# Sixteen channel tiles of a scan computed in the seven-product form, convolved out of SBUF

## The chip, the cores and the metric

One core of a Trainium2 chip runs one program. The metric is the device time of one execution in microseconds (us), median of three runs. All data are fp32.

## The reference, cut to what matters

The program computes three hybrid blocks in a row on 512 tokens with 1024 features. The change lies in the second block's mixer, which computes (gMLP branch, then the state-space branch "ssm"):

```
u          = rmsnorm(h)
za, z, xBC, dt, gates = split(u @ w_in)            # w_in: 1024 x 9248
xBC        = silu(causal_dwconv(xBC, w, b))        # 4 taps per channel, 3072 channels
x, B, C    = split(xBC)                            # x: 2048 channels = 16 tiles of 128
y          = ssd_scan(x, dt, A, B, C) + D * x      # 32 heads of 64 channels, 4 groups for B and C
y          = rmsnorm(y * silu(z))                  # by group
uu, v      = split(gelu(za));  v = spatial mix of layernorm(v)
h          = h + (sigmoid(ga) * ((uu * v) @ w_proj_a) + sigmoid(gb) * (y @ w_proj_b)) @ w_out
```

Here a tile is 128 channels by 512 tokens. A matrix product gives tiles with channels on the partitions; the convolution then runs along the free axis, so tap n adds the tile shifted by n tokens, times a weight per partition.

## The kernel before, in words

**Layout.** Every engine has its own instruction list and they meet at semaphores. `work` is one SBUF arena of 35200 columns, `normalized` holds the eight input tiles of the mixer, `weight_ring` holds four weight slots of 1 MB (two channel tiles, that is 256 output columns, each). SyncE (SP) sends the slots in order; a slot can be sent when the one four before it has been used (`stream.used`).

**Two forms of a product.** In the direct form (`tile_pe`, L2456) one channel tile is 8 products of 128x128 weights with 512 columns. In the seven-product form (class `Sevens`, a Strassen-Winograd scheme on 2x2 blocks; job = two channel tiles) there are 7 products for each of 4 pairs of input tiles: 28 products of 256 columns in place of 32. It needs sums of weight blocks (`sums_pool`, four GpSimd instructions per slot, L999 to L1005; `token_sums_pool`, L1017 to L1022, for two slots at once), sums of input halves (`Halves`, L913 to L933), and sums of the results: `one_act` (a copy on ScalarE, L1110), `three_dve` (L1115), `five_dve` (L1122, L1124) and `all_dve` (L1129). The order of the seven is 1, 2, 6, 5, 7, 3, 4; each half bank is freed by one of these sums. Trace records count each fp32 product as two.

**The second mixer.** After dt (L2530) come eight channel tiles for B and C ("bc", direct form, banks 0 to 2) and their convolution. `convolve_dve` reads the tile from PSUM: one tensor_scalar for the first tap (L3103) and three scalar_tensor_tensor (L3106); ScalarE then applies SiLU (L2857). Then four groups: `group_pe` (L2618, L2619) with a ScalarE copy (L2786) and a masked product on VectorE (L2957); xs tile 0 stands before the first group's instructions, xs tile 1 before the third's.

**The scan's turns.** Sixteen turns follow, one per pair of heads. Turn j has three PE pieces: `turn_pe` (transposes of xs tile j, L2631), `states_pe` (L2640), `outputs_pe` (L2654, L2658). On the others: SP spreads a line of decay sums over the partitions (`spread_line`, L2418, waits for the outputs of turn j-2); GpSimd subtracts (`relative_pool`, 8 instructions, L2752) and multiplies (`weight_pool`, L2762); ScalarE takes two exponentials (`decays_act`, L2878, L2879); VectorE does `aged_dve` (L3144, both inputs in SBUF), `factors_dve` (L3121), `state_dve` (L3128, L3133) and the skip sum (L2981).

**The side work.** Between the three pieces of a turn PE runs pieces of other products, measured in units (one unit is one 256-column product; JOB = 28 units is one job). `share(slot)` says how many units have to be done by each of the 48 slots (3 per turn). The side work is xs tiles 2 to 15 in direct form (16 units each), eight gMLP jobs (`gmlp_u`, `gmlp_v`) and one job of `ssm_z`: 476 units, about 9.9 per slot. `slot_ends` and `job_ends` place the other engines' part of a tile or a job in the slot in which PE ends it, behind that slot's scan instructions. Each engine's list is in this order and is not reordered at run time. GpSimd makes the weight sums of the gMLP jobs in turns 7 to 13. After the scan come 28 more jobs (`DENSE`).

Of the kernel before, what the change touches and what calls it, by code (L numbers as in the profile page):

```python
# [20 lines left out]
P = 128  # L21
# [914 lines left out]
class Sevens:  # L936
# [8 lines left out]
    def __init__(self, K, plans, banks, sums_at, parts_at, made=None, after=None, by_token=()):  # L945
# [9 lines left out]
        self.halfway = take(sum(plan.slots // 2 for plan in by_token)) if by_token else None  # L955
# [23 lines left out]
    def weight_sum(self, n, i):  # L979
        return self.sums_at[n % 2][i]  # L980
# [6 lines left out]
    def sums_pool(self, pool, n, before_last=lambda: None):  # L987
        K, own = self.K, self.K.own_pool.of(pool)
        plan, k = self.slots[n]
        if plan in self.by_token:  # L990
            return self.token_sums_pool(pool, n)
# [15 lines left out]
    def token_sums_pool(self, pool, n):  # L1007
        K, own = self.K, self.K.own_pool.of(pool)
# [3 lines left out]
        s1, s2, s4, s3 = [bass.AP(K.work, first, [[WORK, P], [second - first, 2], [256, 2], [1, 256]]) for first, second in self.sums_at[n]] + (  # L1012
            [a21] if len(self.sums_at[n]) == 3 else [])
        for i in range(2):
            plan.wait_full(pool, 2 * k + i)
# [4 lines left out]
        pool.tensor_tensor(s3, a11, a21, ALU.subtract)  # L1020
        own.wait()
        pool.tensor_tensor(s4, a12, s2, ALU.subtract).then_inc(self.weight_sums.h, 1)  # L1022
# [9 lines left out]
    def token_job_pe(self, pe, j, source, ready):  # L1032
# [5 lines left out]
        for m, p in [(m, p) for m in self.ORDER for p in range(pairs)]:  # L1038
            if p == 0:
                self.bank_free_pe(pe, j, m)  # L1040
                if m == 6:
                    pe.wait_ge(*self.weight_sums(n + 1))
            ready(pe, m, p)
# [1253 lines left out]
TILE = 16  # L2297


class SecondMixer:  # L2300
# [3 lines left out]
    ORDER = (("bc", 8), ("xs", 16))  # L2304
# [3 lines left out]
    def __init__(self, K, d, tables, X, U, plans, sums, norm):  # L2308
# [8 lines left out]
        self.gmlp = Sevens(K, [plans["gmlp_u"], plans["gmlp_v"]], banks, self.gmlp_sums_at, parts, by_token=[plans["gmlp_v"]])  # L2317
        self.dense = Sevens(K, [plans[name] for name in self.DENSE], banks, self.weight_sums_at, parts, self.made, self.gmlp)
# [4 lines left out]
        self.u_first = ApartHalves(U, KD * TM, 0, TM, work, lambda i, p: (self.u_sums + i * 2 * T if i < 3 else self.gv + 6 * T) + p * HALF_BANK)  # L2323
# [9 lines left out]
    def places(self):  # L2333
# [15 lines left out]
        self.gmlp_sums_at = [[self.gv + (3 * (n % 2) + i) * T for i in range(3)] for n in range(4)] + [  # L2349
            [(at, at + T) for at in (self.bt, self.ct, self.cbm)],  # L2350
            [(self.w_t, self.w_t + T), (self.gv + D + T, self.gv + 3 * D + T), (self.ct + 2 * T, self.cbm + 2 * T)]]
        self.gain, self.bias, self.token_bias = (self.bt + 3 * T + i * GMLP_GROUPS * P for i in range(3))
# [6 lines left out]
    def take_signals(self):  # L2359
# [4 lines left out]
            ab0=16 * 8, ab1=16 * 8, first=12, read0=8, read1=8, read2=8, ready=24, grouped=4, copied=4, masked=4,  # L2364
# [3 lines left out]
            u_open=4, v_open=4, u_summed=3, a_summed=1, b_summed=4, out_summed=4).items()}  # L2368
# [13 lines left out]
    def sync(self, sp):  # L2382
# [86 lines left out]
    def side_pe(self, pe, start, stop):  # L2469
        for place in range(start, stop):  # L2470
            yield from self.tile_pe(pe, place)
        for j in range(len(self.gmlp.jobs)):
            source, ready = (self.u_first if j < 4 else self.u_side), {0: self.gmlp_first_pe, 4: self.gmlp_fifth_pe}.get(j, lambda pe, m, p: None)
            for _ in self.gmlp.job_pe(pe, j, source, ready):
                yield 1
        for _ in self.job_pe(pe, "ssm_z", 0):
            yield 1

    def gmlp_fifth_pe(self, pe, m, p):
        if m == 7 and p == 0:  # L2480
            pe.wait_ge(*self.s["u_summed"](3))

    def gmlp_first_pe(self, pe, m, p):
        if m in (1, 2, 5) and p == 0:
            pe.wait_ge(*self.was_read(len(self.tiles) - 3 + (1, 2, 5).index(m)))
# [10 lines left out]
    def share(self, slot):  # L2496

        total = (len(self.tiles) - self.first["xs"] - 2) * TILE + (len(self.gmlp.jobs) + 1) * JOB
# [2309 lines left out]
```

## Time and profile before

| | us |
|---|---|
| three runs: median (lowest to highest) | 3626.12 (3624.08 to 3627.43) |
| profiled execution, its own time | 3630.09 |
| profiled execution, span from first to last instruction | 3628.3 |
| PE busy | 3578.0 |
| VectorE / ScalarE / GpSimd busy | 1599.3 / 761.9 / 1495.8 |
| second mixer, B and C tiles begin | 1601.0 |
| first turn of the scan begins | 1679.2 |
| last side job's sums done, first instruction behind the scan | 1934.4 |

The page of the profile gives busy times over the whole span; the views by group, by wait, by stretch of time and in order of time show the second mixer alone. All times below are microseconds from the start of the span.

### The profile page before, as it was taken

The numbers are of one execution on the slowest core, as the hardware profiler recorded it, in microseconds if no ns is written. First come the engines' busy times: TensorE is split into PE (matmuls) and PEld (weight loads), VectorE is DVE, ScalarE is ACT, GpSimd is POOL, SyncE is SP. The second block draws the span as 40 slices with busy tenths as digits, with TensorE's granted clock in tenths as the row PEclk, the third lists the DMA queues.
The fourth block names the chain that finished last, engine by engine and source line by source line (L and its number), as shares of the span: only waits on it lengthen the run. The fifth ranks groups of instructions, "written<-read, shape, count | busy, mean of one in ns | idle before, by whom it ended". The sixth has DMA issues, their size and how long they took to land.

```text
span 3628.3 us, 45688 instructions
## 1 busy us (share of the span) xinstructions
PE 3578.0 (99%) x18937; PEld 2880.3 (79%) x18937; DVE 1599.3 (44%) x2456; ACT 761.9 (21%) x1378; POOL 1495.8 (41%) x1248
## 2 busy tenths in 40 slices
PE   8999999999999999999999999999999999899999
PEld 7888888775888888864588888888887468658888
DVE  3221222422436322135656633688623554358851
ACT  2000151223211100012334300100102454320000
POOL 4454222000645355414686664366630111026653
PEclk9999999999999999999999999999999999999999
DMA  4232444423332323231333222232223400023322
GB/s 135 82 93 75 87 70 66 74 47 76 60 74 82 93 82 91 87 99 59 105 105 100 82 82 93 82 93 82 87 87 102 81 24 5 6 78 85 90 79 76
DMA packets 370386, 286.30 MB, mean 79 GB/s; under 512 B 11283, under 2 KB 360083, under 8 KB 370180
## 3 DMA queue, kind: packets, MB, share of 16 engines
q1 hardware_dynamic: 367876, 279.44, 29.2%
q10 hardware_dynamic: 2304, 3.95, 0.4%
q8 instruction: 150, 2.46, 0.3%
q14 instruction: 56, 0.46, 0.0%
HBM read 280.64 MB, written 2.72 MB: 78 GB/s over the span
## 4 chain that ended last, share of the span: by engine, by line
PE 97%; DVE 1%; ACT 1%; issue 1%; DMA 1%; SPq 0%; DVEq 0%; ACTq 0%
PE psum L618 43%; PE psum L1078 20%; PE psum L2456 4%; PE psum L1044 3%; PE psum L3500 3%; PE psum L1704 2%; PE psum L1739 2%; PE psum L1465 2%; PE psum L4338 2%; PE psum L4073 1%; PE psum L587 1%; PE psum L3584 1%; PE psum L3604 1%; PE psum L1725 1%; PE psum L1580 1%; PE psum L3457 1%
## 5 line engine op out<-in xcount | busy, mean ns | idle before, releaser
L618 PE MATMUL psum<-work 128*128 128x256 f32 (+1 forms) x2400 | 551.4, 381 | 0.0
L537 POOL TENSOR_TENSOR work<-weight_ring 128x512 f32<-128x512 f32 x132 | 163.3, 1237 | 912.6 <-PE psum L618 732.9
L618 PEld LDWEIGHTS psum<-work 128*128 128x128 f32 x2400 | 455.9, 190 | 66.1 <-DVE work L751 0.2
L618 PE MATMUL psum<-work,weight_ring 128*128 128x256 f32 (+1 forms) x2080 | 481.8, 381 | 0.0
L618 PE MATMUL psum<-normalized,weight_ring 128*128 128x256 f32 (+1 forms) x2016 | 468.1, 382 | 3.0 <-DVE normalized L738 3.0
L618 PEld LDWEIGHTS psum<-work,weight_ring 128*128 128x128 f32 x2080 | 395.2, 190 | 57.2
L618 PEld LDWEIGHTS psum<-normalized,weight_ring 128*128 128x128 f32 x2016 | 383.8, 190 | 61.2 <-DVE normalized L738 4.3
L762 DVE TENSOR_TENSOR work<-work,psum 128x512 f32<-128x512 f32 (+1 forms) x100 | 68.6, 686 | 641.4 <-PE psum L618 641.4
L1078 PE MATMUL psum<-work,weight_ring 128*128 128x256 f32 x1216 | 283.6, 379 | 0.0
L1078 PE MATMUL psum<-work 128*128 128x256 f32 x1184 | 277.1, 379 | 0.0
L696 ACT ACTIVATE work<-psum 128x256 f32<-128x256 f32 (+1 forms) x100 | 38.5, 385 | 1094.4 <-PE psum L618 1094.4
L1078 PEld LDWEIGHTS psum<-work,weight_ring 128*128 128x128 f32 x1216 | 230.4, 190 | 31.9 <-issue 0.9
L1078 PEld LDWEIGHTS psum<-work 128*128 128x128 f32 x1184 | 224.6, 190 | 33.7 <-issue 3.7
L799 DVE SCALAR_TENSOR_TENSOR work<-work,vector_columns 128x510 f32<-128x510 f32 (+1 forms) x176 | 223.7, 1329 | 0.0
L999 POOL TENSOR_TENSOR work<-weight_ring 128x512 f32<-128x512 f32 x60 | 79.9, 1331 | 332.0 <-PE psum L1078 288.2
L542 POOL TENSOR_TENSOR work<-weight_ring,work 128x512 f32<-128x512 f32 x132 | 185.2, 1403 | 0.0
L540 POOL TENSOR_TENSOR weight_ring<-weight_ring 128x512 f32<-128x512 f32 x132 | 174.4, 1321 | 0.0
L539 POOL TENSOR_TENSOR work<-work,weight_ring 128x512 f32<-128x512 f32 x132 | 168.1, 1274 | 10.3
L2456 PE MATMUL psum<-normalized,weight_ring 128*128 128x512 f32 x384 | 170.0, 595 | 0.0
L1078 PE MATMUL psum<-normalized,weight_ring 128*128 128x256 f32 x704 | 163.5, 380 | 0.0
L618 PE MATMUL psum<-normalized,work 128*128 128x256 f32 (+1 forms) x672 | 159.9, 381 | 0.0
L1078 PEld LDWEIGHTS psum<-normalized,weight_ring 128*128 128x128 f32 x704 | 132.9, 190 | 19.4 <-issue 1.9
(556 smaller groups left out, 5317.6 us busy)
## 6 DMA issues: line engine op xcount, KB each, us to landing
weight_ring<-in_w_in SPq DMA_DIRECT2D x73, 1024.0 KB, 7.9
weight_ring<-in_w_ffn_in SPq DMA_DIRECT2D x88, 512.0 KB, 5.1
weight_ring<-in_ffn_w_up SPq DMA_DIRECT2D x44, 512.0 KB, 4.8
weight_ring<-in_ffn_up SPq DMA_DIRECT2D x44, 512.0 KB, 5.1
weight_ring<-in_w_ffn_out SPq DMA_DIRECT2D x16, 1024.0 KB, 5.2
weight_ring<-in_w_out SPq DMA_DIRECT2D x12, 1024.0 KB, 5.1
work<-decay_sums SPq DMA_DIRECT2D x16, 512.0 KB, 4.2
weight_ring<-in_w_proj_b SPq DMA_DIRECT2D x8, 1024.0 KB, 5.2
```

Of the source, the lines that this page charges most:

```text
L537: own(pool.tensor_tensor(s1, a21, a22, ALU.add))
L539: own(pool.tensor_tensor(s2, s1, a11, ALU.subtract))
L540: pool.tensor_tensor(a21, a11, a21, ALU.subtract)
L542: pool.tensor_tensor(s4, a12, s2, ALU.subtract).then_inc(self.weight_sums.h, 1)
L618: last = pe.matmul(K.ps[:, self.BANK[m] * T:self.BANK[m] * T + self.H], left(m, p), right(pe, m, p), start=first and p == 0, stop=last_par ...
L799: last = dve.scalar_tensor_tensor(out=acc[ct][:, n:T], in0=raw[ct][:, 0:T - n], scalar=weight[ct][n], in1=acc[ct][:, n:T], op0=ALU.mult, o ...
L999: own(pool.tensor_tensor(s1, a21, a22, ALU.add))
L1044: last = pe.matmul(self.half_bank(m), source.right(m, p)[:, t * P:(t + 1) * P], self.token_left(plan, k, n, m, p), start=p == 0 and m in ( ...
L1078: last = pe.matmul(self.half_bank(m), self.left(plan, k, n, m, p), source.right(m, part * pairs + p), start=first and p == 0 and m in (1, ...
L1465: last = pe.matmul(K.bank(b + h, HALF), plan.slot(k)[:, kt, ct * P:(ct + 1) * P], U[:, at:at + HALF], start=kt == 0, stop=kt == KD - 1)
L2456: last = pe.matmul(self.bank_of(place), plan.slot(k)[:, kt, ct * P:(ct + 1) * P], src[:, kt * stride:kt * stride + T], start=kt == 0, stop ...
L3500: last = pe.matmul(K.bank(4 + n % 3), plan.slot(k)[:, kt, ct * P:(ct + 1) * P], self.U[:, kt * TM:kt * TM + T], start=kt == 0, stop=kt == ...
```

## The change

All sixteen xs tiles become eight jobs of the seven-product form, in front of the gMLP jobs in one list (`self.side`, 16 jobs). Job j's four quarters go to a buffer of two tiles in SBUF (`raw`) by the usual result sums. ScalarE then computes the first tap with the bias (`begin_act`, Identity with scale and bias, from `raw` into the tile), VectorE adds the three other taps from `raw` (`taps_dve`, scalar_tensor_tensor with both tensors in SBUF, six per job), and ScalarE applies SiLU (`xs_silu_act`). Weight sums of the eight slots are added on GpSimd: slots 0 to 2 ahead of turn 0, slot j+2 in turn j up to turn 9, between `relative_pool` and `weight_pool`; the two token sums are split in two parts each. PE does 10 units of job 0 before group 0, 10 before group 2, and the rest of job 0 and 14 units of job 1 behind group 3 (`AHEAD` = 42 units) before turn 0; the remaining 434 units are spread over the 48 slots. SP sends the line of pair j behind weight slot j+2 (before: j+1).

```diff
-TILE = 16
+AHEAD = JOB + 14
-    ORDER = (("bc", 8), ("xs", 16))
+    ORDER = (("bc", 8),)
-        self.gmlp = Sevens(K, [plans["gmlp_u"], plans["gmlp_v"]], banks, self.gmlp_sums_at, parts, by_token=[plans["gmlp_v"]])
+        self.side = Sevens(K, [plans[name] for name in ("xs", "gmlp_u", "gmlp_v")], banks, self.side_sums_at, parts, by_token=[plans["gmlp_v"]])
+        self.raw = self.gu + 6 * T
@@ sync
-            if i - 1 < SSM_PAIRS:
-                self.spread_line(sp, i - 1)
+            if 3 <= i - 2 < SSM_PAIRS:
+                self.spread_line(sp, i - 2)
@@ PE
-    def side_pe(self, pe, start, stop):
-        for place in range(start, stop):
-            yield from self.tile_pe(pe, place)
...
+    def side_pe(self, pe):
+        for j in range(len(self.side.jobs)):
+            for _ in self.side.job_pe(pe, j, self.u_side, self.first_side_pe if j == 0 else lambda pe, m, p: None):
+                yield 1
+    def first_side_pe(self, pe, m, p):
         if m in (1, 2, 5) and p == 0:
+            pe.wait_ge(*self.was_read({1: 6, 2: 7, 5: 5}[m]))
@@ share, job_ends
+        return AHEAD - (-(slot + 1) * ((len(self.side.jobs) + 1) * JOB - AHEAD) // (3 * SSM_PAIRS))
+        events = dict(one=4, three=12, five=20, all=28, begin=29, open=30, taps=38, silu=46)
@@ tensor
         for g in range(SSM_GROUPS):
             if g % 2 == 0:
-                for _ in self.tile_pe(pe, xs + g // 2):
-                    pass
+                self.side_until(side, (g + 2) // 2 * 10)
             self.group_pe(pe, g)
+        self.side_until(side, AHEAD)
@@ gpsimd
+        self.relative_pool(pool, 0)
+        G.sums_pool(pool, 0)
+        pool.wait_ge(*self.plans["bc"].done(3))
+        self.u_side.last_sum(pool, 0, KD // 2).then_inc(S["u_summed"].h, 1)
+        G.sums_pool(pool, 1)
+        G.sums_pool(pool, 2)
+        self.weight_pool(pool, 0)
+        for j in range(1, SSM_PAIRS):
             self.relative_pool(pool, j)
+            if j <= 9:
+                G.sums_pool(pool, j + 2)
...
             self.weight_pool(pool, j)
@@ scalar
+    def begin_act(self, act, j):
+        S = self.s
+        act.wait_ge(*self.side.read_all(j + 1))
+        for i in range(2):
+            t = 2 * j + i
+            act.activation(self.A(self.xs + t * T, T), self.A(self.raw + i * T, T), ACT.Identity, scale=self.V("ssm_conv_w_2")(3 * 24 + t),
+                           bias=self.V("ssm_conv_b_2")(t)).then_inc(S["begun"].h, 1)
@@ vector
+        self.side_dve(dve, own, "all", 0)
+        self.side_dve(dve, own, "taps", 0)
         self.aged_dve(dve, 0)
+    def taps_dve(self, dve, own, j):
+        for i in range(2):
+            t = 2 * j + i
+            x, raw = self.A(self.xs + t * T, T), self.A(self.raw + i * T, T)
+            dve.wait_ge(*self.s["begun"](t + 1))
+            for n in range(1, 4):
+                step = dve.scalar_tensor_tensor(out=x[:, n:T], in0=raw[:, 0:T - n], scalar=self.V("ssm_conv_w_2")((3 - n) * 24 + t), in1=x[:, n:T],
+                                                op0=ALU.mult, op1=ALU.add)
+                if n < 3:
+                    own(step)
+                    own.wait()
+                else:
+                    step.then_inc(self.s["convolved"].h, 1)
```

## Rows read from the trace of the kernel before

**Rows 1.** The page: busy time and share of the span of each engine.
```profile
PE 3578.0 (99%) x18937; PEld 2880.3 (79%) x18937; DVE 1599.3 (44%) x2456; ACT 761.9 (21%) x1378; POOL 1495.8 (41%) x1248
```

**Rows 2.** Busy time by stretch: the groups, a turn with xs tiles, two with jobs.
```profile
core 0: us, PE busy (x) PEld busy (x) DVE busy (x) ACT busy (x) POOL busy (x), PEclk, DMA share, GB/s
1650.00:1700.00 50.00, 45.55 (x176) 24.29 (x175) 27.37 (x39) 11.67 (x15) 13.33 (x14) 1.00 0.15 53
1713.43:1729.29 15.86, 15.86 (x69) 8.19 (x68) 10.43 (x17) 5.83 (x6) 7.85 (x9) 1.00 0.31 94
1839.64:1855.57 15.93, 15.93 (x99) 13.89 (x98) 7.37 (x12) 4.62 (x5) 14.68 (x13) 1.00 0.28 95
```

**Rows 3.** Waits of PE, 1660 to 1940: total, times, longest.
```profile
PE psum L2631 <- ACT work L2786: 2.3, 1, 2.3
PE psum L2640 <- DVE work L3121: 2.2, 1, 2.2
```

**Rows 4.** The chain that ended last: start, length, what.
```profile
1667.43 6.88 PE psum L2456 x16
...
1860.50 0.67 PE psum L2640 x6
...
2024.53 12.09 PE psum L1078 x56
```

**Rows 5.** VectorE in order of time: the convolution of the last bc tile.
```profile
1657.95 0.81 DVE L3103 TENSOR_SCALAR work<-psum,vector_columns 128x512 f32<-128x512 f32 x1 [3.71 <-PE psum L2456]
1658.79 2.31 DVE L3106 SCALAR_TENSOR_TENSOR work<-psum,vector_columns,work 128x511 f32<-128x511 f32 x3
```

**Rows 6.** One line's instructions: duration in ns, min/median/max, first and last start.
```profile
L3106 DVE SCALAR_TENSOR_TENSOR work<-psum,vector_columns,work x72: 746/748/751, 1612.4 to 1802.5; 128x511 f32<-128x511 f32 x24, 128x510 f32<-128x510 f32 x24, 128x509 f32<-128x509 f32 x24
L799 DVE SCALAR_TENSOR_TENSOR work<-work,vector_columns x176: 734/1215/1756, 2342.7 to 3498.4; 128x511 f32<-128x511 f32 x88, 128x510 f32<-128x510 f32 x88
L3144 DVE TENSOR_TENSOR work<-work x16: 1214/1902/2547, 1682.6 to 1911.4; 128x1024 f32<-128x1024 f32 x16
L2762 POOL TENSOR_TENSOR work<-work x16: 2352/2358/2366, 1681.6 to 1909.6; 128x1024 f32<-128x1024 f32 x16
L2752 POOL TENSOR_SCALAR work<-work x128: 704/712/1687, 1640.1 to 1907.7; 128x128 f32<-128x128 f32 x128
L999 POOL TENSOR_TENSOR work<-weight_ring x60: 1265/1271/2256, 463.9 to 2296.7; 128x512 f32<-128x512 f32 x60
```

**Rows 7.** VectorE and GpSimd in order of time in turn 9.
```profile
1832.32 2.36 POOL L2762 TENSOR_TENSOR work<-work 128x1024 f32<-128x1024 f32 x1 [1.17 <-ACT work L2878]
1833.22 2.54 DVE L3144 TENSOR_TENSOR work<-work 128x1024 f32<-128x1024 f32 x1 [1.99 <-ACT work L2879]
1834.63 2.26 POOL L999 TENSOR_TENSOR work<-weight_ring 128x512 f32<-128x512 f32 x1
```

**Rows 8.** The feed-forward block's convolution from SBUF beside GpSimd's weight sums.
```profile
2507.55 3.42 DVE L799 SCALAR_TENSOR_TENSOR work<-work,vector_columns 128x511 f32<-128x511 f32 x2
2507.31 1.44 POOL L540 TENSOR_TENSOR weight_ring<-weight_ring 128x512 f32<-128x512 f32 x1
2508.72 1.72 POOL L542 TENSOR_TENSOR work<-weight_ring,work 128x512 f32<-128x512 f32 x1
2510.39 1.18 POOL L550 TENSOR_TENSOR work<-work 128x256 f32<-128x256 f32 x1
```

**Rows 9.** VectorE groups by line and shape: busy, mean ns, idle before.
```profile
L1115 DVE TENSOR_TENSOR work<-work,psum 128x512 f32<-128x512 f32 x60 | 41.1, 685 | 166.9 <-PE psum L1078 131.8 <-PE psum L1044 29.6 <-ACT work L1110 5.4
L1129 DVE TENSOR_TENSOR work<-work,psum 128x512 f32<-128x512 f32 x52 | 35.7, 686 | 75.8 <-PE psum L1078 64.2 <-PE psum L1044 11.0
L2981 DVE SCALAR_TENSOR_TENSOR work<-work,psum 128x512 f32<-128x512 f32 x16 | 11.8, 740 | 4.7 <-PE psum L2658 4.7
L3121 DVE TENSOR_TENSOR work<-psum,work 128x512 f32<-128x512 f32 x32 | 20.5, 682 | 10.6 <-PE psum L2631 10.6
```

**Rows 10.** Waits of GpSimd, 1640 to 1940: total, times, longest.
```profile
POOL work L2752 <- DMA work<-decay_sums: 33.9, 10, 6.5
```

More of the change, by code:

```diff
@@ L954, in __init__ @@
         self.read_all = take(self.results)
-        self.halfway = take(sum(plan.slots // 2 for plan in by_token)) if by_token else None
+        self.halfway, self.token_sums = (take(sum(plan.slots // 2 for plan in by_token)) if by_token else None for _ in range(2))
     def job(self, plan, c=0):
@@ L2496, in share @@
     def share(self, slot):
-        total = (len(self.tiles) - self.first["xs"] - 2) * TILE + (len(self.gmlp.jobs) + 1) * JOB
-        return -(-(slot + 1) * total // (3 * SSM_PAIRS))
-    def slot_ends(self):
-        start, stop = self.first["xs"] + 2, len(self.tiles)
-        out = {}
-        for n, place in enumerate(range(start, stop)):
-            out.setdefault(self.slot_of((n + 1) * TILE), []).append(place)
-        return out
+        return AHEAD - (-(slot + 1) * ((len(self.side.jobs) + 1) * JOB - AHEAD) // (3 * SSM_PAIRS))
     def slot_of(self, unit):
@@ L2512, in job_ends @@
     def job_ends(self, kinds):
-        first = (len(self.tiles) - self.first["xs"] - 2) * TILE
-        out = sorted((first + j * JOB + at, kind, j) for j in range(len(self.gmlp.jobs))
-                     for kind, at in dict(one=4, three=12, five=20, all=28, open=30).items() if kind in kinds)
+        events = dict(one=4, three=12, five=20, all=28, begin=29, open=30, taps=38, silu=46)
+        skip = lambda kind, j: kind == "open" if j < 8 else kind in ("begin", "taps", "silu")
+        out = sorted((j * JOB + at, kind, j) for j in range(len(self.side.jobs)) for kind, at in events.items()
+                     if kind in kinds and not skip(kind, j) and j)
         return [(self.slot_of(unit), kind, j) for unit, kind, j in out]
@@ L2868, in gelu_act @@
         A, S = self.A, self.s
-        act.wait_ge(*self.gmlp.read_all(j + 1))
+        act.wait_ge(*self.side.read_all(8 + j + 1))
         at = self.gmlp_at(j)[0]
@@ L2962, in vector @@
         own.wait()
+        self.side_dve(dve, own, "all", 0)
+        self.side_dve(dve, own, "taps", 0)
         self.aged_dve(dve, 0)
-        ends, jobs = self.slot_ends(), self.job_ends(("three", "five", "all"))
+        ends = self.job_ends(("three", "five", "all", "taps"))
         for slot in range(3 * SSM_PAIRS):
@@ L2972, in vector @@
                 self.aged_dve(dve, j + 1)
-            for place in ends.get(slot, []):
-                self.convolve_dve(dve, own, place)
-            for at, kind, job in jobs:
+            for at, kind, job in ends:
                 if at == slot:
-                    self.gmlp_dve(dve, kind, job)
+                    self.side_dve(dve, own, kind, job)
             if slot % 3 == 2:
@@ L3049, in open_dve, with side_dve @@
             dve.tensor_tensor(y, y, A(self.result(j) + (t % 2) * T, T), ALU.mult).then_inc(S["opened"].h, 1)
-    def gmlp_dve(self, dve, kind, j):
-        G, (c11, c12, c21, c22) = self.gmlp, self.gmlp_at(j)
+    def side_dve(self, dve, own, kind, j):
+        G = self.side
+        c11, c12, c21, c22 = self.gmlp_at(j - 8) if j >= 8 else [self.raw + i * HALF_BANK for i in range(4)]
         if kind == "three":
```

127 lines of the change are left out of this document (66 added, 61 removed).

## Prediction

> **What bounds the kernel now.** I read the page first, then the stretches, the waits, the chain and the instructions in order of time. The page shows PE busy for 3578.0 of 3628.3 us [rows 1]; in the stretches of the scan it is busy for the whole of 15.86 and 15.93 us, at the full granted clock [rows 2]. So a turn costs what PE has to issue in it, and the other engines cost nothing as long as they deliver in time. The only waits of PE between the B and C tiles and the end of the scan are 2.28 us at the first transposes and 2.18 us at the first states [rows 3], the 4.45 us that PE is short in 1650 to 1700 [rows 2]. The reader should see a second thing in the same rows: in a turn with jobs GpSimd is busy for 14.68 of 15.93 us, in one with xs tiles for 7.85 of 15.86 [rows 2]. VectorE has 7.4 to 10.4 us.
>
> **PE's products.** A tile in direct form takes 6.88 us, a job of two tiles 12.09 [rows 4]. Two tiles become one job: 2 x 6.88 - 12.09 = 1.67 us, times eight: 13.4 us off PE. Clock and weight loads stay as they are in both rows.
>
> **The head.** Both waits of [rows 3] go, since PE now has 22 units behind group 3: -4.46. A new one comes: the second product of job 0 takes bank 1, which VectorE reads until the last B/C tile is convolved. That convolution ends 0.2 + 0.81 + 2.31 us and small gaps, some 3.4, behind the tile's last product [rows 5]; PE has four units, 1.73 us, to cover it: +1.7. Net -2.8. Behind this wait stand only PE's own groups, which nobody needs earlier. Weight sum 0 and both halves' sums are made on GpSimd while the B/C tiles run, so product 6 doesn't wait.
>
> **The turns, PE alone.** A unit is 12.09 / 28 = 0.432 us. A turn with jobs has 99 records in 15.93 us; 38 are its own (4, 6 and 28), the rest is 30 units: 12.95. So its own pieces cost 2.98. With 434 / 16 = 27.1 units the new turn is 14.69 us, and from the end of one job to the end of the next (28 units) PE needs 14.69 x 28 / 27.1 = 15.2. That is no further gain, only the same 13.4 told by turns; it is the pace that the others must keep.
>
> **ScalarE.** Per job one copy, two first taps and two SiLUs are some 3 us; it has 4.6 to 5.9 us per turn now [rows 2]. Far from the bound, and the first tap moved there takes 2 x 0.81 us off VectorE. Nothing on the path.
>
> **SP.** The line of pair j goes one slot later in SP's list. The send in front of it waits for job j-2, which ends before the outputs that the line waits for anyway. GpSimd waits for such lines now, up to 6.5 us, ten times [rows 10], and PE waits for nothing: cost 0. If the cover went, it would be that wait less GpSimd's slack.
>
> **GpSimd.** Per turn 8 x 0.70 + 2.36, plus four weight sums of 1.27: 5.6 + 2.4 + 5.1 = 13.0 us of 14.7 [rows 6]. Before, turns 0 to 6 had only 7.9. That fits, if nobody holds it up.
>
> **VectorE's taps are the term that decides.** Read alone, a tap from PSUM is 0.748 us and one with both inputs in SBUF 0.734 at its shortest [rows 6]: even. But the second kind has a median of 1.215 and a maximum of 1.756 [rows 6]. Rows 7 and 8 show why. An instruction of VectorE with two inputs in SBUF waits while GpSimd works on SBUF and the other way round: L3144 (1.21 alone) took 2.54, ending 1.1 us behind L2762; L999 (1.27 alone) took 2.26, since it stood behind L3144 [rows 7]. Where both have a queue they alternate: two taps in 3.42 us beside L540 and L542, which grow to 1.44 and 1.72 [rows 8], so 1.68 from tap to tap. VectorE's evictions (one input in PSUM) keep 0.685 [rows 9]. The 42 PSUM taps of the scan's tiles were immune to this; the new 48 SBUF taps aren't. Their prices: 1.68 beside a 128x512 sum; beside L2762 0.73 + 2.36 less the overlap of 0.33 that 1.68 against 0.74 + 1.27 shows, 2.8; beside L2752 0.73 + 0.71 - 0.33 = 1.1.
>
> What stands beside them: the end of job j releases VectorE's last sum of it and GpSimd's weight sums for slot j+2 at once. VectorE does that sum (0.68) and `aged_dve` (1.21, with a wait 1.6), then six taps; GpSimd is by then in its second or third sum, and goes on to L2762 and the eight L2752. So three taps at 1.68, one at 2.8, two at 1.1: 10.1 us instead of 4.6.
>
> **The loop.** Behind the taps stand, on the same engine, the first sum of the next job (0.64), the skip sum (0.74) and the two instructions of `factors_dve` (1.28) [rows 9]; PE's `states_pe` waits for these. It is 0.67 [rows 4], and behind it job j+1 lacks 5 (j = 0) to 11 (j = 7) units: states of turn j come at unit 51 + 27.1j, the job ends at 56 + 28j. At eight that is 3.45. Round: 0.68 + 1.6 + 10.1 + 0.64 + 0.74 + 1.28 + 0.67 + 3.45 = 19.2 us, against 15.2 that PE needs. PE stalls 4.0 us per job, in front of `states_pe` or `outputs_pe`, for the eight jobs with taps: +32. From turn 8 on there are none, and the turn is 14.7.
>
> **Sum.** -13.4 - 2.8 + 32 = +15.8. The profiled execution's 3630.1 becomes 3645.9; its own time is 4.0 above the median of the runs, so 3642.
>
> **The bounds of the tap.** At 0.73 each (plus handover 0.04) the loop is 13.3 us, under 15.2, and PE doesn't stall. It begins to stall at 1.0 us per tap, and the change comes out even at a stall of 2.0, that is 1.35 per tap. The mean over all 176 of L799 is just 1.33, but the feed-forward stages leave GpSimd free for half of each job (that is where the 0.734 come from), while here it has work for 13.0 of 14.7 us. So I take the contended prices. At the upper end nothing overlaps: 0.74 + 1.27 = 2.0, 3.1 and 1.45, 12.0 per job: 1.9 more per job, +15.
>
> **Two rules of the Trainium skill.** Rows 8 show alternation with a third of a microsecond of overlap per pair. The page "SBUF — State Buffer", section "Who interferes with whom", calls the shared interface an exclusive lock held for the whole instruction; by that each pair would be 2.0 and the time some 15 us longer; the trace's 1.68 decides for me, and the rule is the heavier rival. Against me, "VectorE: DVE Perf Modes" of the Trainium skill, section "Rules for kernel authors", advises to take a matmul's output to SBUF first where many operations follow, and its section on the TRN2 errata gives an SBUF source 62 cycles less of fixed cost than a PSUM source. By it a tap would be an estimated 0.065 us cheaper than before, and the change would end at the first rival's time; rows 6 show 0.014 cheaper alone and up to 1.0 dearer beside GpSimd.
>
> **Rivals.**
> 1. *The taps find the interface free* (faster). For it: in rows 6 a third or so of L799 runs near its shortest, and a faster engine can fall into step. Against: both engines start at the same event, and GpSimd has 88% of the turn. All gain stays: 3630.1 - 16.2 - 4.0 = 3610. Chance 0.14.
> 2. *Taps at the mean of L799, 1.33* (no change): loop 17.1, stall 1.9, +15 - 16.2: 3625. Chance 0.17.
> 3. *Whole-instruction lock* (much slower), decided from the point where taps beside a 128x512 sum are 2.0: also GpSimd itself then has 13.0 + 6 x 0.73 + 1.2 = 18.6 per turn, late with L2762, and PE waits in front of `outputs_pe`. 3642 + 15 = 3657. Chance 0.15.
> 4. *The change doesn't shorten PE's list*, if the eight jobs' products or their waits on the weight sums ran slower than those of the gMLP jobs. Rows 4's 12.09 is from the same code, so within rival 2's chance.
> The forecast itself 0.54.
>
> **Numbers.** Time 3642. The range leaves out most of rival 1 and the far side of 3: 3616 to 3658. Within 0.2% (7.3 us, about what a measurement of this kernel tells from none) I count most of rival 2: 0.13; faster 0.20 (rival 1 and the lower part of 2); slower 0.67. The forecast alone: 3634 to 3650.
>
> **What would show it.** Right: PE's share falls to about 9 tenths in the scan's first half, with waits of 3 to 5 us at L2640 for L3121 in turns 0 to 5; tap instructions with a median over 1.5 us; turns of 18 to 19 us up to turn 7, then 14.7. Wrong: turns of 14.7 from the start and taps at 0.73 (rival 1); waits of PE in front of `outputs_pe` for L2762 in every turn (rival 3); waits of PE for weight sums, which I put at nothing; job periods other than 12.09 us of products.

## The result and the profile after

The changed kernel is slower by 0.4%: 3643.5 us (median of 5 runs, 3639.0 to 3645.5) against 3626.8 (5 runs, 3624.1 to 3629.7), ratio 1.0042, 95% interval 1.0029 to 1.0055. The forecast was 3642, range 3616 to 3658. The profiled execution took 3643.04 us with a span of 3641.2, 12.9 more than the one of before. The sum came out right, but by luck: the largest term was twice what came, and costs that stand nowhere in the sum made up for it.

The page of the changed kernel, busy time by engine:

```profile
PE 3572.5 (98%) x19129; PEld 2919.3 (80%) x19129; DVE 1634.1 (45%) x2472; ACT 778.2 (21%) x1403; POOL 1551.1 (43%) x1279
```

PE's busy time falls by 5.5 us against [rows 1] and not by 13.4; the part on the clock comes back to that.

Busy time by stretch, the counterpart of [rows 2]: the groups with the head of the scan, 19.2 us from the first transposes of turn 3 on (the turn has 17.9 of them), and 14.6 us of turns 9 and 10, as long as each of these is:

```profile
core 0: us, PE busy (x) PEld busy (x) DVE busy (x) ACT busy (x) POOL busy (x), PEclk, DMA share, GB/s
1650.00:1700.00 50.00, 46.11 (x249) 37.92 (x249) 32.36 (x38) 17.79 (x23) 32.59 (x24) 1.00 0.16 49
1734.80:1754.00 19.20, 16.21 (x102) 13.86 (x101) 17.17 (x21) 7.94 (x10) 16.52 (x15) 1.00 0.35 105
1839.80:1854.40 14.60, 14.60 (x94) 12.71 (x93) 6.32 (x11) 3.56 (x4) 13.31 (x13) 1.00 0.38 124
```

A turn that PE alone sets is 14.6 us (14.69 forecast), GpSimd is busy for 13.3 of it (13.0 forecast). In the 19.2 us PE isn't busy for 3.0 and VectorE is for 17.2. The head lacks 3.9 us of PE now, 4.45 before: it gained 0.6, not 2.8. By the first transposes (L2629) the turns 0 to 14 are 16.4, 17.5, 19.2, 17.9, 17.7, 19.9, 14.8, 18.2, 15.1, 14.6, 14.6, 20.7, 14.6, 14.6 and 14.6 us.

PE's waits, 1600 to 1980: total, times, longest (in answer to [rows 3]):

```profile
PE psum L2638 <- DVE work L3157: 18.0, 7, 3.3
PE psum L2652 <- DVE work L3169: 1.9, 1, 1.9
PE psum L1092 <- DVE work L3142: 1.5, 1, 1.5
PE psum L2629 <- ACT work L2876: 1.3, 1, 1.3
```

L2638 is the product for the states (L2640 before), L3157 is `factors_dve` (L3121 before), L2652 the outputs. The seven waits of the first row stand in turns 0 (about 1.0), 1 to 5 (2.6 to 3.3 each) and 11 (2.8).

VectorE's taps and the aged product, duration in ns, min/median/max, first and last start, against the L799 and L3144 of [rows 6]; and the taps by shape (busy us, mean ns):

```profile
L3089 DVE SCALAR_TENSOR_TENSOR work<-work,vector_columns x48: 748/1562/2841, 1676.0 to 1813.4; 128x511 f32<-128x511 f32 x16, 128x510 f32<-128x510 f32 x16, 128x509 f32<-128x509 f32 x16
L3180 DVE TENSOR_TENSOR work<-work x16: 1219/1792/3658, 1685.2 to 1930.0; 128x1024 f32<-128x1024 f32 x16
```

```profile
L3089 DVE SCALAR_TENSOR_TENSOR work<-work,vector_columns 128x511 f32<-128x511 f32 x16 | 30.0, 1875 | 0.9 <-ACT work L2869 0.9
...
L3089 DVE SCALAR_TENSOR_TENSOR work<-work,vector_columns 128x510 f32<-128x510 f32 x16 | 19.3, 1206 | 0.6
L3089 DVE SCALAR_TENSOR_TENSOR work<-work,vector_columns 128x509 f32<-128x509 f32 x16 | 18.4, 1150 | 0.6
```

Together 67.7 us, 8.5 per job of six taps, 1.41 each. The first tap of each tile is the dear one, 1.88.

One loop in order of time, turns 3 and 4, VectorE, GpSimd, and of PE the two stalls:

```profile
1746.33 0.69 DVE L1143 TENSOR_TENSOR work<-work,psum 128x512 f32<-128x512 f32 x1 [1.78 <-PE psum L1092]
1746.93 1.80 DVE L3180 TENSOR_TENSOR work<-work 128x1024 f32<-128x1024 f32 x1
1748.66 9.43 DVE L3089 SCALAR_TENSOR_TENSOR work<-work,vector_columns 128x511 f32<-128x511 f32 x6
1758.00 0.74 DVE L3001 SCALAR_TENSOR_TENSOR work<-work,psum 128x512 f32<-128x512 f32 x1
1758.66 1.28 DVE L3157 TENSOR_TENSOR work<-psum,work 128x512 f32<-128x512 f32 x2
```

```profile
1746.37 1.28 POOL L1000 TENSOR_TENSOR work<-weight_ring 128x512 f32<-128x512 f32 x1 [2.60 <-PE psum L1092]
1747.73 2.13 POOL L1002 TENSOR_TENSOR work<-work,weight_ring 128x512 f32<-128x512 f32 x1
1749.83 1.71 POOL L1003 TENSOR_TENSOR weight_ring<-weight_ring 128x512 f32<-128x512 f32 x1
1751.50 1.71 POOL L1006 TENSOR_TENSOR work<-weight_ring,work 128x512 f32<-128x512 f32 x1
1753.17 2.79 POOL L2766 TENSOR_TENSOR work<-work 128x1024 f32<-128x1024 f32 x1
```

```profile
1742.26 0.94 PE L2638 MATMUL psum<-work 128*128 128x128 f32 x6 [2.99 <-DVE work L3157]
...
1759.99 0.38 PE L2638 MATMUL psum<-work 128*128 128x128 f32 x1 [2.83 <-DVE work L3157]
```

Both engines start at the end of the job's last product (1746.33 and 1746.37). GpSimd's first sum takes 1.28, the next three 2.13, 1.71 and 1.71 where one alone takes 1.27, and its multiply 2.79 instead of 2.36 [rows 6]; the six taps take 9.4. From the states of turn 3 to those of turn 4 it is 17.7 us, of which PE waits for 2.8.

**The clock.** The forecast has no term for this. Behind some stalls PE runs at half its clock for a while. Busy time by stretch around four such places (columns as above; the clock is the last but two):

```profile
1724.00:1728.00 4.00, 4.00 (x13) 3.21 (x12) 0.93 (x5) 2.00 (x2) 0.19 (x1) 0.57 0.00 0
...
1779.00:1783.00 4.00, 4.00 (x14) 3.27 (x14) 2.26 (x7) 2.00 (x2) 1.28 (x2) 0.61 0.00 0
1816.00:1820.00 4.00, 3.96 (x31) 3.52 (x32) 2.12 (x3) 3.14 (x3) 0.81 (x2) 0.57 0.00 0
1874.00:1881.00 7.00, 6.04 (x17) 5.15 (x18) 2.73 (x8) 4.79 (x6) 6.92 (x8) 0.52 0.00 0
```

They stand behind the waits of turn 2 (2.6), turn 5 (3.3), turn 7 (1.9, at the outputs) and turn 11 (2.8). A mean clock of 0.57 over 4 us loses 4 x 0.43 = 1.7 us; the four rows lose 1.7 + 1.6 + 1.7 + 3.4 = 8.4 us. In the last of them 0.3 falls in time in which PE was still waiting (its row begins at 1874, the product at 1874.96), so 8.1 cost time, 3.0 of these in turn 11. The kernel before has no such place in the scan. That is also why PE's busy time fell by 5.5 only: -13.4 + 8.1 = -5.3, since a product at half clock is busy for longer.

**The account.** It is drawn up for the stretch from the first product for B and C to the first instruction behind the scan. Before, that is 333.4 us (1601.0 to 1934.4). After, its first and last row are

```profile
1598.23 4.99 PE L2470 MATMUL psum<-normalized,weight_ring 128*128 128x512 f32 x11
...
1946.97 1.04 PE L2665 MATMUL psum<-identity,work 128*128 128x128 f32 x8
```

which makes 348.7: +15.3. Ahead of it this execution was 2.8 us faster than the one of before. I don't put that down to the change: the kernels below that have the changed kernel's code up to this point get there between 1598.5 and 1601.6. Behind it the two differ by 0.3. So the 12.9 between the two spans is 2.4 too kind to the change; the medians differ by 16.7.

The terms in this stretch: products -13.4; head -0.6; waits of turns 1 to 5, 14.2; of the outputs in turn 7, 1.9; of turn 11, 2.8; clock 8.1; and some 0.26 behind each of the seven waits for `factors_dve`, by which the turns are longer than 14.64 and the wait together (turn 3 is 17.90, with a wait of 2.99): 1.8. Together +14.8, against 15.3.

### The profile page after: what moved, and what is told of

Its sections match the earlier page's. It is cut to its first block, busy times and chain, and to the rows that moved or that the text cites. A ratio compares the mean times of both kernels' runs of the same rounds, so it can differ in the third digit from the quotient of the medians.

```text
span 3641.2 us, 46190 instructions
## 1 busy us (share of the span) xinstructions
PE 3572.5 (98%) x19129; PEld 2919.3 (80%) x19129; DVE 1634.1 (45%) x2472; ACT 778.2 (21%) x1403; POOL 1551.1 (43%) x1279
## 4 chain that ended last, share of the span: by engine, by line
PE 94%; DVE 4%; issue 1%; ACT 1%; POOL 0%; DMA 0%; DVEq 0%; SPq 0%; ACTq 0%; POOLq 0%
PE psum L618 43%; PE psum L1092 20%; PE psum L1058 3%; PE psum L3536 3%; PE psum L1718 2%; PE psum L1753 2%; PE psum L4374 2%; PE psum L1479 2%; PE psum L2470 2%; DVE work L3089 1%; PE psum L4109 1%; PE psum L587 1%; PE psum L3620 1%; PE psum L3640 1%; PE psum L1594 1%; PE psum L1739 1%
## 5 line engine op out<-in xcount | busy, mean ns | idle before, releaser
L537 POOL TENSOR_TENSOR work<-weight_ring 128x512 f32<-128x512 f32 x132 | 163.2, 1236 | 912.1 <-PE psum L618 731.5
L618 PEld LDWEIGHTS psum<-work 128*128 128x128 f32 x2400 | 455.9, 190 | 66.7 <-DVE work L751 0.9
L618 PEld LDWEIGHTS psum<-work,weight_ring 128*128 128x128 f32 x2080 | 395.2, 190 | 57.2
L618 PEld LDWEIGHTS psum<-normalized,weight_ring 128*128 128x128 f32 x2016 | 382.8, 190 | 61.0 <-DVE normalized L738 4.4
L1092 PE MATMUL psum<-work 128*128 128x256 f32 x1312 | 307.0, 379 | 0.0
L1092 PE MATMUL psum<-work,weight_ring 128*128 128x256 f32 x1248 | 293.9, 381 | 0.0
L1092 PEld LDWEIGHTS psum<-work 128*128 128x128 f32 x1312 | 248.4, 190 | 36.3 <-issue 3.3
L1092 PEld LDWEIGHTS psum<-work,weight_ring 128*128 128x128 f32 x1248 | 237.7, 191 | 34.1 <-issue 1.9
L1000 POOL TENSOR_TENSOR work<-weight_ring 128x512 f32<-128x512 f32 x68 | 88.7, 1305 | 367.4 <-PE psum L1092 324.9
L799 DVE SCALAR_TENSOR_TENSOR work<-work,vector_columns 128x510 f32<-128x510 f32 (+1 forms) x176 | 223.6, 1328 | 0.0
L1092 PE MATMUL psum<-normalized,weight_ring 128*128 128x256 f32 x928 | 218.0, 381 | 1.5 <-DVE work L3142 1.5
L1092 PEld LDWEIGHTS psum<-normalized,weight_ring 128*128 128x128 f32 x928 | 174.7, 190 | 27.2 <-issue 2.5
L1352 POOL TENSOR_TENSOR work<-work 128x512 f32<-128x512 f32 x8 | 10.1, 1266 | 312.6 <-PE psum L1642 268.9
```

What stands on the lines that cost most here:

```text
L537: own(pool.tensor_tensor(s1, a21, a22, ALU.add))
L618: last = pe.matmul(K.ps[:, self.BANK[m] * T:self.BANK[m] * T + self.H], left(m, p), right(pe, m, p), start=first and p == 0, stop=last_par ...
L799: last = dve.scalar_tensor_tensor(out=acc[ct][:, n:T], in0=raw[ct][:, 0:T - n], scalar=weight[ct][n], in1=acc[ct][:, n:T], op0=ALU.mult, o ...
L1000: own(pool.tensor_tensor(s1, a21, a22, ALU.add))
L1092: last = pe.matmul(self.half_bank(m), self.left(plan, k, n, m, p), source.right(m, part * pairs + p), start=first and p == 0 and m in (1, ...
```

## Experiments

My theory: the long taps come from GpSimd alone, through VectorE's second input in SBUF; PE's stalls come from the taps; and the clock is lost by the stalls. Rivals: the taps are long for another reason (SBUF traffic, the program order); VectorE's load as such; something else in the change costs the time. The kernel before was timed anew beside each group of experiments, and each ratio below is to that time: 3628.6 us beside the kernels without taps, with one input, with the taps in two places and with the quarters; 3627.7 beside those two together, the two of the order and the first filled head; 3628.6 beside the rest. For traces I give the stretch of the account too (333.4 before, 348.7 after), since it leaves out what varies elsewhere; it is one execution each.

**No taps, or taps with one input.** The first kernel leaves the three taps out, the second has an instruction of the same 512 columns with a single SBUF input in each one's place.

```diff
-                step = dve.scalar_tensor_tensor(out=x[:, n:T], in0=raw[:, 0:T - n], ..., in1=x[:, n:T], ...)
+                step = dve.bn_stats(self.A(self.stats + 6 * (3 * t + n - 1), 6), raw)
```

> Leaves out the three VectorE taps of the sixteen xs tiles (48 instructions); everything else as in the changed kernel, so the scan works on tiles with only the first tap. Theory A (the taps and GpSimd hold each other up at the shared SBUF interface) and theory B (VectorE simply has too many instructions between aged and factors) both expect PE's waits for factors to go: turns of 14.7 us throughout the first half, no stretch at the lower clock there, 3643.5 - 21 - 8 = about 3614. Theory C (the weight sums added to GpSimd make it late, whatever VectorE does) expects most of the waits to stay: above 3630.

> In place of each tap stands a batch_norm_stats over the same 512 columns: one SBUF input instead of two, about as long when alone (some 0.7 us), same waits and same place in the list; its result is not used, so taps 1 to 3 are missing from the output. Theory A: it isn't held up beside GpSimd, six take 4.5 us instead of 8.5, the turns are 14.7 and the time is within 3 us of the kernel without taps (3614). Theory B (count and length of instructions): stays within 5 us of 3643.

Measured: 3615.4 us for both (ratios to before 0.9966, 0.9953 to 0.9979, and 0.9964, 0.9952 to 0.9977). The instructions of the second kernel, in ns:

```profile
L3089 DVE BATCH_NORM_STATS2 work<-work x48: 676/694/699, 1676.9 to 1789.3; 128x6 f32<-128x512 f32 x48
```

48 of them beside the same GpSimd work, and none above 0.70 us. All turns but turn 11 are 14.6 or 15.1, the waits of turns 0 to 5 are gone, and no clock is lost in turns 0 to 10. So everything else in the change (two more ScalarE passes, GpSimd's sums, the order of the lines) is free but for one wait in turn 11, and the two-input taps cost 3643.5 - 3615.4 = 28.1 us, where I had put +32 (28.5 by the stretch, which is 320.2 without taps; 30 if each time is taken against the kernel before beside it). The new instruction also writes less, 6 columns in place of 512. That this isn't what saves it is shown by an instruction of the changed kernel that writes 512 columns to SBUF beside the same GpSimd work, with one of its inputs in PSUM:

```profile
L3001 DVE SCALAR_TENSOR_TENSOR work<-work,psum x16: 733/740/746, 1703.2 to 1943.1; 128x512 f32<-128x512 f32 x16
```

The Trainium skill's page "SBUF — State Buffer", section "Who interferes with whom", says that a VectorE instruction with at most one SBUF input doesn't contend with GpSimd, and one with two does; both agree with this pair. What is left in the second kernel is one wait, in turn 11:

```profile
PE psum L2638 <- DVE work L3156: 2.8, 1, 2.8
PE psum L1092 <- DVE work L3141: 1.5, 1, 1.5
```

**GpSimd silent beside the taps.**

```diff
-            if j <= 9:
+            if j <= 5:
+                plan, k = G.slots[j + 2]
+                plan.wait_full(pool, k)
+                pool.wait_ge(*G.passed(j))
+                pool.sem_inc(G.weight_sums.h, 1)
+            elif j <= 9:
                 G.sums_pool(pool, j + 2)
```

> The changed kernel with GpSimd's four weight sums of slots 3 to 7 left out (turns 1 to 5; the products read old sums, so their values are not the reference's; PE's work, VectorE's and ScalarE's is whole). It is the same question as in e2, asked from the other side: there the taps were made immune, here GpSimd is silent beside them. My theory: the long taps are GpSimd's doing, so the taps that run in those turns (about 24 of 48) fall from a median of 1.56 to near 1.1 us or below (0.7 to 0.8 where no other GpSimd instruction lies beside them), PE's waits at the product for the states in turns 1 to 5, now 15 of 18 us, fall to under 3, the granted clock has no low stretch before turn 8, and the time comes to about 3628 (15 of waits less 3 left, and some 5 of clock less: 3643.5 - 12 - 4). Rival: the taps are long because VectorE reads and writes SBUF three times over beside ScalarE and the DMA queues; then their mean stays above 1.3 in those turns and the time above 3638.

Measured: 3621.4 us (0.9981, 0.9972 to 0.999). The taps between 1700 and 1770, the turns without GpSimd's sums, in ns:

```profile
L3094 DVE SCALAR_TENSOR_TENSOR work<-work,vector_columns x25: 737/749/837, 1699.8 to 1759.0; 128x509 f32<-128x509 f32 x9, 128x511 f32<-128x511 f32 x8, 128x510 f32<-128x510 f32 x8
```

25 taps, none above 0.84. GpSimd stands still beside most of them: in turn 1 from 1709.00 to 1713.99, where the six taps run from 1710.01 to 1714.55. Turns 1 to 5 are 14.6 with no wait at L2638, and no clock is lost before turn 11. The time is 6.6 us better than I wrote. The stretch is 22.0 shorter than the changed kernel's: 14.2 of waits and the 1.3 behind them, 3.4 of the clock in turns 2 and 5, and 3.1 of the clock in turns 7 and 11, where the waits are as long as before (1.9 and 2.8) and the clock fell not at all or for a shorter time. These 3.1 aren't the doing of the experiment as far as its trace shows. With the pair above this settles the cause of the stalls from both sides: make the tap immune, or make GpSimd silent, and they are gone.

**Taps in two places.** The six taps of a job, which all start beside GpSimd's sums, are parted: three in the slot of unit 33, three in that of unit 45.

```diff
-        events = dict(one=4, three=12, five=20, all=28, begin=29, open=30, taps=38, silu=46)
+        events = dict(one=4, three=12, five=20, all=28, begin=29, open=30, taps0=33, silu0=40, taps1=45, silu1=52)
```

> The same computation; the taps of a job's second tile are moved some twelve units later, so that on VectorE the first sum of the next job and a slot's scan instructions can come between the two tiles' taps. Theory A with the loop of the prediction: only three contended taps stand in front of factors, the stall per job falls from 2.65 to about 1 us (VectorE has some 15.7 us of work per turn against 14.7) and with it the stretches at the lower clock: 3618 to 3630. If it is GpSimd's lateness that decides, the order on VectorE changes nothing: 3640 or more.

Measured: 3628.9 (0.9999, 0.9989 to 1.0008). Taps in ns, and PE's waits:

```profile
L3091 DVE SCALAR_TENSOR_TENSOR work<-work,vector_columns x48: 735/832/2834, 1679.4 to 1805.0; 128x511 f32<-128x511 f32 x16, 128x510 f32<-128x510 f32 x16, 128x509 f32<-128x509 f32 x16
```

```profile
PE psum L2638 <- DVE work L3159: 10.8, 9, 2.8
PE psum L1092 <- DVE work L3144: 1.5, 1, 1.5
...
```

The median falls from 1.56 to 0.83. The waits at L2638 fall by 7.2 us, to none above 1.7 in turns 0 to 10, and no clock is lost in the scan: 7.2 + 1.5 of outputs + 8.1 = 16.8, against 16.3 by the stretch (332.4). Between the medians it is 14.6, or 16.4 with each taken against the kernel before beside it. Of the 8.1 from the clock, 3.0 stand in turn 11, where the wait is still 2.8: this execution's clock didn't fall behind it, and the parted taps can't be the reason.

**Shorter instructions on GpSimd.** The multiply by the mask (128x1024) in four pieces of 256 columns.

```diff
-        pool.tensor_tensor(seg, seg, same(A(self.cbm + (j // 4) * T, T), 2), ALU.mult).then_inc(S["weighted"].h, 1)
+        for q in range(4):
+            seg, H = A(self.seg + (j % 2) * 2 * T + q * HALF_BANK, HALF_BANK), HALF_BANK
+            last = pool.tensor_tensor(seg, seg, A(self.cbm + (j // 4) * T + (q % 2) * H, H), ALU.mult)
+        last.then_inc(S["weighted"].h, 1)
```

> The same computation; GpSimd's multiply of 128x1024 per turn (2.36 us) is cut into four of 128x256. Theory A, with a lock held per instruction: the tap that falls beside it waits 0.5 us instead of up to 2.3, so one tap per job gets 1 to 1.5 us shorter, GpSimd gets some 0.3 us more per turn; 3630 to 3638. Theory B: unchanged, 3643. A third possibility, that GpSimd keeps the interface over instructions that follow without a gap: unchanged or slower, since the tap waits for all four.

> Taps in two places and the weight multiply in quarters together, same computation. If the two act on different waits (order in front of factors; length of one instruction that a tap waits for), the second still takes off about half of its 5 us: 3624 to 3628. If both only took away the same stalls: 3629, as the first alone.

Measured: 3638.3 (1.0027, 1.0017 to 1.0036) alone, and 3630.5 (1.0011, 1.0002 to 1.0021) with the parted taps. Alone, the taps' median is 1.15 and the waits at L2638 are 17.0, seven times: the taps get shorter by 0.14 on average, but GpSimd's four pieces take 4.6 us together where the one took 2.8 (with no taps beside them, from 1841 on, four take 2.8 too, and one 2.36). That its work then reaches further into the taps that were free is my reading, no run parts it. With parted taps the waits are 13.2 instead of 10.8, and the time is above both values I had thought possible. So shorter instructions on GpSimd gave a few us alone (3638.3 against 3643.5), with 17.0 of 18.0 us of waits left, and took some away with the parted taps; they aren't the lever.

**The order of things in three places.** The parted taps, job 0's taps parted as well, and the third of the token weights' sums behind the relative decays of turn 11; then all of it with the quarters.

```diff
+    def third_token_sum_pool(self, pool, n):
+        a11, _, a21, _, _, _, s3, _ = self.token_parts(n)
+        pool.tensor_tensor(s3, a11, a21, ALU.subtract).then_inc(self.weight_sums.h, 1)
             elif j == 11:
+                G.third_token_sum_pool(pool, 12)
                 G.last_token_sum_pool(pool, 12)
```

> Taps in two places, and the same split for job 0 (second tile's taps behind the first factors), and the third token sum moved behind the next turn's subtraction on GpSimd (turn 11's wait of 2.8 us is put down to this sum standing in front of it). Same computation. Turn 11 at 14.7 instead of 17.7 and 2 us less at turn 0: 3628.9 - 3 - 2 = 3623 to 3625. If turn 11's wait has another cause: 3626 to 3628.

> The three changes of order of the run before and the weight multiply in quarters: 3618 to 3623 if they add up, which beats the kernel before (3626.8); 3623 to 3627 if the quarters bring nothing any more.

Measured: 3627.6 (1.0000, 0.999 to 1.0009) and 3631.1 (1.001, 1.0 to 1.0019); the second missed both of its values. In the first the wait of turn 11 stayed at 2.8. Why, stands in the order of time there, first VectorE, then GpSimd:

```profile
1855.54 5.98 DVE L3192 TENSOR_TENSOR work<-work 128x1024 f32<-128x1024 f32 x1 [4.89 <-ACT work L2906]
```

```profile
1853.44 2.37 POOL L1018 TENSOR_TENSOR weight_ring<-weight_ring 128x1024 f32<-128x1024 f32 x1
1855.77 2.36 POOL L1036 TENSOR_TENSOR work<-weight_ring,work 128x1024 f32<-128x1024 f32 x1
1858.07 2.36 POOL L2772 TENSOR_TENSOR work<-work 128x1024 f32<-128x1024 f32 x1
```

The aged product, about 1.2 us long alone, stands from 1855.54 to 1861.5: through the rest of one GpSimd instruction and the whole of two more that follow with no wait between them. In the changed kernel it is the same with one such pair, the last token sum and the multiply: 3.66 us, and PE's 2.8 of turn 11. It was the change that put the one right ahead of the other. I hadn't forecast it; nor do the taps have a part in it, since the kernel without taps has it too.

**A gap between two GpSimd instructions.** The parted taps, and GpSimd waits for its own last token sum before it goes on to the multiply; then the same ahead of each turn's multiply.

```diff
                 G.last_token_sum_pool(pool, 12)
+                pool.wait_ge(*G.token_sums(1))
```

> The kernel with the taps in two places (e4, 3628.85) and one wait more: in turn 11 GpSimd, between the last sum of the token weights and the multiply by the mask, waits for its own sum to be finished, so that the two 128x1024 instructions no longer follow each other without a gap. Theory: VectorE's two-input multiply of the aged state lost its turn there (3.65 us where 1.1 is its own length) because the second GpSimd instruction was already queued behind the first. With the gap it gets in between: it takes under 2.3 us, PE's wait of 2.8 in turn 11 falls below 1, and the time falls by 1.5 to 2.5, to about 3626.8. Rival: the order does not depend on a gap; VectorE's instruction stays at 3.6 and the time at 3628.9.

> As the last, with the same wait ahead of the multiply by the mask in each of turns 1 to 10 as well. Theory: the aged multiply's mean falls from about 1.8 to 1.5 us or less, because it mostly arrives while a sum runs and then gets in ahead of the 2.35 us multiply; GpSimd's multiply comes up to 1.1 later, which has slack. PE's waits for the states in turns 2 to 8 (8 us in e4) fall to about 5, the time to 3624. Rival: the aged multiply seldom meets that pair except in turn 11, and the time stays at that of the last kernel, within 1 us; or the later multiply by the mask is waited for at the outputs, and it is slower.

Measured: 3627.5 (0.9995, 0.9986 to 1.0004) and 3625.5 (0.9992, 0.9983 to 1.0001). Turn 11 of the first:

```profile
1856.86 1.34 DVE L3183 TENSOR_TENSOR work<-work 128x1024 f32<-128x1024 f32 x1 [7.20 <-ACT work L2899]
```

```profile
1854.76 2.37 POOL L1031 TENSOR_TENSOR work<-weight_ring,work 128x1024 f32<-128x1024 f32 x1
1857.20 3.23 POOL L2767 TENSOR_TENSOR work<-work 128x1024 f32<-128x1024 f32 x1
```

The two instructions are 0.07 us apart instead of back to back, and the aged product slips in: 1.34 us where it took 3.65 with the same taps. GpSimd's multiply pays 0.87 for it. PE's wait in turn 11 falls from 2.8 to 0.5, the turn from 17.7 to 15.4 us. That part of the theory is shown, at this one place. The whole time moved by 1.3 us, which these intervals can't tell from nothing (the stretch is 330.3 against 332.4). In every turn the gap does no more: the aged product's mean goes from 1.84 to 1.76, not to the 1.5 I expected, and the waits stay (8.6 and 8.9).

**The other half of the change alone: the head of the kernel before filled.** One xs tile more before turn 0; then the same, with the fourth token sum counted apart.

```diff
+        self.side_until(side, TILE)
-        return -(-(slot + 1) * total // (3 * SSM_PAIRS))
+        return TILE - (-(slot + 1) * (total - TILE) // (3 * SSM_PAIRS))
```

> The kernel before with one thing of the change alone: PE does one xs tile (16 units) between group 3 and turn 0, the rest is spread over the 48 slots as before. The two waits at the head (2.28 and 2.18 us) should go or nearly so: 3622 to 3624. If what stands behind them (VectorE's convolution of that tile in front of factors) takes their place: 3626 to 3628, no change.

> The kernel before with the idle time ahead of turn 0 filled (e7, 3626.92) and the token weights' fourth sum counted apart from the third, so that the product that reads sums 1 and 2 no longer waits for the fourth (the wait of 2.3 us that e7 got in return). Theory: the 4.5 us at the head that e7 removed were lost again at this wait and the 1.7 us of half clock behind it; with the wait gone (the third sum ends 2.35 us earlier, just when PE asks) and no low clock in the scan the time is 3626.9 - 2.3 - 1.7 = 3622.9, below both kernels. Rival: a later point takes it back once more (the stream of weights, or the chain of the scan, which in e7 still showed turns of 15.0 to 16.5); then the span of the scan is shorter and the whole time within 1 us of 3627.

Measured: 3626.9 (0.9996, 0.9987 to 1.0005) and 3625.7 (0.9994, 0.9985 to 1.0003). The 4.5 us of [rows 3] are gone in both (PE is busy for all of 1650 to 1700). In the first a new wait of 2.3 came at the token products, with 0.28 of the clock gone in the 6 us behind it (1.7 us), and the stretch is what it was (333.3): the time without gain that I had named, but for another reason. In the second there is none, and no clock lost in the scan, but two waits at the states, 1.5 us in all:

```profile
PE psum L2647 <- DVE work L3128: 1.5, 2, 1.1
```

Its profiled span is 6.2 us shorter than before's, but only 2.5 of these lie in the stretch (330.9); the medians differ by 2.9, within what they can tell from none, and the time lies between the two values I had given.

## Why the prediction was right

- *Products, -13.4:* held. A turn that PE alone sets took 14.6 (14.69 forecast), and PE's busy time agrees once the clock is taken out.
- *Head, -2.8:* came to -0.6. The new bank wait was 1.5 (1.7 forecast), but the first transposes still waited 1.3, for the SiLU of job 0, and the first states 1.0: the taps of job 0 stand in front of turn 0, which I had not counted. It is my step "both waits go" that failed, in size.
- *ScalarE and SP, 0:* held, by the kernel with one-input instructions, but for that first SiLU. *GpSimd 13.0:* 13.3.
- *Taps, 10.1 us per job:* right mechanism, a little too dear: 9.4 for jobs 2 to 5, 8.5 on average. In the loop shown the six took 1.75, 1.64, 1.64, 2.83, 0.75 and 0.75: three at the price of [rows 8], one at that of the multiply, as forecast; the last two, beside the subtractions, took what they take alone where I had 1.1.
- *The loop, 19.2:* 18.3 and 18.2 from the end of one job to the end of the next (1728.00 to 1746.33 to 1764.49), where PE needs 15.2. The taps are 0.7 of the difference. In the second of these loops the next job's first sum ran behind `factors_dve` and not in front of it, as the rows show.
- *The stall, 4.0 eight times, +32:* five of 2.6 to 3.3 in turns 1 to 5, one of 1.9 at the outputs in turn 7. That is the term that was mis-sized: 16.1 against 32 (17.1 with turn 0's). Of the 16 too much 5.8 are in the size of the five in turns 1 to 5, the rest in the number: job 0's taps stand in front of turn 0, and in turns 6 and 7 the taps start behind `factors_dve` (at 1792.11 and 1806.93, the factors at 1790.90 and 1805.72), so the states don't wait for them, and they take 5.4 and 7.2 us for six.
- *Not in the sum at all:* the clock after the stalls, 8.1; the wait of turn 11, 2.8 ("from turn 8 on there are none" was wrong); the 1.8 behind the waits. The taps' whole cost of 28 is made of the stalls (16.1), the two waits of the head that are theirs (1.3 and 1.0), what stands behind the waits (0.26 six times) and the clock (8.1). The wait of turn 11 isn't in it, for it is there without taps; the clock's 3.0 behind it is, and that part is chance, since the same wait had no such price in the kernel without taps. So the forecast's +32 came near because 16 us too much in the stalls and the missing terms nearly cancel. That is luck in the number; the mechanism, taps and GpSimd's sums in turns and PE waiting for `factors_dve`, is what came.
- *The heavier rival, the whole-instruction lock:* the taps beside queued sums took 1.7 a pair, not 2.0, so its price was wrong here. But its rule is what one sees in turn 11, where the aged product was shut out through the rest of one GpSimd instruction and the whole of the next, which follows without a gap. The Trainium skill's page "SBUF — State Buffer" says in the section "Who interferes with whom" that issue order decides who blocks; in turn 11 the trace agrees, where a gap of 0.07 us let VectorE go first. A gap isn't needed everywhere: some of the sums beside which the taps alternate follow each other as closely (L1003 to L1006 above), and so do L2762 and L999 of [rows 7], between which the aged product got in. What makes the difference stays open.
- *Rival 2, taps at 1.33:* the nearest in the tap's price (1.41 measured), yet its time, 3625, is 18 us off: its 15 us of stalls are about what came, and the clock, turn 11, the head and the 1.8 are missing.

No version that computes the reference ran clearly below both kernels: the three nearest (gap in each turn, gap in turn 11, head filled twice) have intervals that reach 1. The seven-product form itself is worth 13 us here; its taps from SBUF take 28, and parted and with a gap they still take 10 to 12 of these (3625.5 and 3627.5 against 3615.4).

## What to carry to other kernels

Before an operand moves from PSUM to SBUF, ask what GpSimd does at that time: a two-input VectorE instruction that costs the same alone (0.748 us from PSUM, a median of 0.749 from SBUF without the sums) cost nearly twice as much beside GpSimd's queue (1.41), and one with a single SBUF input cost nothing more. Price a stall of PE with what can follow it: here seven waits of 1.9 to 3.3 us brought 8.1 us of clock on top, four of them with such a loss and three without, and none of the waits shorter than 1.9 in any of these scans had one. Where a long GpSimd instruction stands right ahead of another and VectorE is late, try a wait between the two before shorter instructions; at the one place where it was tried it took 2.3 us off a turn. And compare one stretch in two traces, not two spans: the spans here hide 2.4 us of the change.

## What the hardware did that I hadn't expected

- The granted clock fell to half (1.2 of 2.4 GHz) behind some stalls and not behind others of the same length: behind turn 2's 2.6 us it fell, behind the 3.0 of turn 3 it didn't. The price was 1.6 to 1.7 us at three places and 3.0 at turn 11. That wait of 2.8 stands with the same length in six of the profiled kernels; behind it the clock fell in four (the changed one, with one input, without GpSimd's sums, with the order of three) and stayed whole in two (without taps, with taps in two places). In order of time of PE there, eight equal products at half and, later, at full clock:

```profile
1878.11 3.40 PE L1058 MATMUL psum<-weight_ring,normalized 128*128 128x256 f32 x8
```

The same eight take 1.89 at full clock.
- An own wait of 0.07 us on GpSimd turned 3.65 us of a VectorE instruction into 1.34.
- GpSimd pays for the contention as well: four pieces of 256 columns took 4.6 us beside the taps and 2.8 with nobody beside them, one of 1024 took 2.8 and 2.36.
